# A two-block transformer kernel: norm sums joined, latent projections in full tiles, small tables loaded last

## What is computed

```python
# first block, each layer l
h = x @ w_in[l]                      # split into fox, latent (cq, ckv, kr), stick-breaking and windowed parts
q = (_rmsnorm(cq, g_q) @ w_uq).reshape(B, S, 4, 64 + 32)      # cq: 256 wide
kv = (_rmsnorm(ckv, g_kv) @ w_ukv).reshape(B, S, 4, 64 + 64)  # ckv: 128 wide
q = concat([q[..., :64], _rope(q[..., 64:], cos, sin)])       # then causal attention at scale 96 ** -0.5
y = _group_rmsnorm(mix, mix_g[l]) @ w_o[l]
x = _layernorm(ALPHA * x + y, ln1_g[l], ln1_b[l])
f = (silu(x @ w_gate[l]) * (x @ w_up[l])) @ w_down[l]         # 2816 wide
x = _layernorm(ALPHA * x + f, ln2_g[l], ln2_b[l])
# second block, each layer: half a SwiGLU, a mixer (differential attention with a bucketed
# relative bias, a short convolution, a gated linear recurrence), another half SwiGLU, RMS norms
```

## Time and profile before

| what | value |
|---|---|
| median of three runs | 3189.45 us (3188.94 to 3190.36) |
| the profiled execution's own time | 3188.79 us |
| its span | 3187.0 us |
| PE busy | 3149.3 us, 99% |
| POOL busy | 2284.4 us, 72% |
| DVE busy | 1169.8 us, 37% |
| ACT busy | 707.8 us, 22% |
| granted TensorE clock, mean | 0.998 |

### The profile page before, as it was taken

How to read it: one execution, slowest core, us unless ns; L and a number is a source line. 1 busy time by engine, 2 the same in 40 slices (tenths; PEclk the granted TensorE clock), 3 DMA queues, 4 the chain that set the end, 5 groups by cost and what they waited for, 6 DMA issues and landing times.

```text
span 3187.0 us, 45061 instructions
## 1 busy us (share of the span) xinstructions
PE 3149.3 (99%) x15738; PEld 2613.2 (82%) x15738; DVE 1169.8 (37%) x1874; ACT 707.8 (22%) x1444; POOL 2284.4 (72%) x3079
## 2 busy tenths in 40 slices
PE   8999999999999999999999999999999999999999
PEld 7778888887788888888888788888888887788887
DVE  5576111255761112542226552222222227542211
ACT  3453111044531110311102321110111012321100
POOL 5335877764358777598877478887888877398884
PEclk9999999999999999999999999999999999999999
DMA  5111322222113222232233122232322232132221
GB/s 182 47 41 60 112 93 98 96 90 67 41 54 106 98 98 93 71 108 95 96 99 103 60 80 99 99 99 93 99 92 99 99 109 86 41 106 99 93 98 66
DMA packets 83017, 284.08 MB, mean 89 GB/s; under 512 B 9531, under 2 KB 15068, under 8 KB 82652
## 3 DMA queue, kind: packets, MB, share of 16 engines
q1 hardware_dynamic: 77632, 274.76, 25.9%
q10 hardware_dynamic: 5276, 7.73, 0.7%
HBM read 278.79 MB, written 3.67 MB: 89 GB/s over the span
## 4 chain that ended last, share of the span: by engine, by line
PE 67%; POOL 19%; issue 13%; DVE 1%; POOLq 1%; ACT 0%; DMA 0%; SPq 0%; DVEq 0%; ACTq 0%
PE bank_v L512 14%; PE bank_v L514 14%; PE bank_v L513 14%; POOL w_lo L486 10%; PE bank_a L512 6%; PE bank_a L514 6%; PE bank_a L513 6%; POOL w_hi L484 6%; POOL zero L483 3%; PE bank_s L974 1%; PE bank_a L810 1%; PE bank_s L849 1%; PE bank_v L989 1%; PE bank_v L831 0%; PE bank_s L977 0%
## 5 line engine op out<-in xcount | busy, mean ns | idle before, releaser
L486 POOL TENSOR_TENSOR w_lo<-raw,w_hi 128x512 fp32r<-128x512 f32 x1024 | 1421.1, 1388 | 82.2
L483 POOL TENSOR_TENSOR zero<-zero 128x1 f32<-128x1 f32 x1024 | 288.8, 282 | 789.2 <-PE bank_v L514 606.8
L512 PE MATMUL bank_v<-xn_hi,w_hi 128*128 128x512 f32 (+1 forms) x1696 | 646.5, 381 | 14.4 <-DVE xn_lo L1640 12.1
L484 POOL CAST w_hi<-raw 128x512 fp32r<-128x512 f32 x1024 | 647.8, 633 | 0.0
L514 PE MATMUL bank_v<-xn_hi,w_lo 128*128 128x512 f32 (+1 forms) x1696 | 638.5, 376 | 0.0
L513 PE MATMUL bank_v<-xn_lo,w_hi 128*128 128x512 f32 (+1 forms) x1696 | 638.2, 376 | 0.0
L512 PE MATMUL bank_a<-xn_hi,w_hi 128*128 128x512 f32 (+1 forms) x1248 | 473.6, 379 | 8.4 <-DVE xn_lo L1640 5.4
L513 PE MATMUL bank_a<-xn_lo,w_hi 128*128 128x512 f32 (+1 forms) x1248 | 469.8, 376 | 0.0
L514 PE MATMUL bank_a<-xn_hi,w_lo 128*128 128x512 f32 (+1 forms) x1248 | 469.6, 376 | 0.0
L512 PE MATMUL bank_v<-h_hi,w_hi 128*128 128x512 f32 (+1 forms) x1122 | 423.7, 378 | 0.0
L513 PE MATMUL bank_v<-h_lo,w_hi 128*128 128x512 f32 (+1 forms) x1122 | 422.5, 377 | 0.0
(11 more groups left out here) (354 smaller groups left out, 3174.2 us busy)
## 6 DMA issues: line engine op xcount, KB each, us to landing
raw<-in_w_stream SPq DMA_DIRECT2D x516, 512.0 KB, 3.3
resid<-in_x SPq DMA_DIRECT2D x8, 256.0 KB, 9.1
rope<-in_rope ACTq DMA_DIRECT2D x2, 1024.0 KB, 6.1
da_v<-t_rows ACTq DMA_DIRECT2D x2, 1024.0 KB, 7.5
out<-resid SPq DMA_DIRECT2D x8, 256.0 KB, 2.3
t_rows<-t_row ACTq DMA_DIRECT2D x1, 1536.0 KB, 6.5
mla_v<-in_alibi ACTq DMA_DIRECT2D x2, 512.0 KB, 7.2
work<-in_lru_w ACTq DMA_DIRECT2D x2, 256.0 KB, 3.0
```

What stands on the lines that cost most here:

```text
L483: pool.tensor_tensor(zero[:, 1:2], zero[:, 0:1], zero[:, 0:1], ALU.add)
L484: pool.tensor_copy(w_hi[:, u, cut], raw[:, u, cut]).then_inc(*hi_split.done(("unit", u, n)))
L486: ins = pool.tensor_tensor(w_lo[:, u, cut], raw[:, u, cut], w_hi[:, u, cut].bitcast(F32), ALU.subtract)
L512: pe.matmul(out, lhs_hi, rhs_hi, start=first, stop=False)
```

## The change

It has five parts.

1. The six small tables are no longer issued by ACT at its start but by SP, behind the twelve loads of `HEAD` and ahead of the weight stream.
2. The weights of `uq` are laid out anew on the host, so that four outputs of 128 rows hold a head's 64 plain, 32 rotary and 32 turned rows; `uk` is formed as two outputs of two heads each. The scaling of the plain rows moves from DVE to ACT; DVE keeps cosine and sine for each head, and ACT copies both halves of each `uk` bank.
3. The shift is scaled by the matrix itself: `shift_weights` (-1/256, a memset of DVE at each norm) stands in place of `ones`, the operation L1802 is gone, and `base` and the centring of chunks 0 and 1 read the shift from PSUM.
4. For the first half DVE adds chunk 7 to both sums (two operations more, 128x256), and `ln_stats(tag, 0)` has four one-column matmuls in place of eight. The second half keeps its number.
5. Places: in `project_out` the spread of half 0 comes one step k (three matmuls) earlier; in `down` the sums of half 0 stand one step later (f = 4) and their spread one earlier (f = 8); in `project_halves` the second half's sums stand after n = 3 and its spread after n = 5. In the apply loop DVE's eviction of chunk 7's second half comes after step 4, and ACT's square of it after step 3.

```diff
-        ln_shift, ln_sum, ln_squares, ln_square = overlay(
+        shift_weights, _, ln_sum, ln_squares, ln_square = overlay(
...
+            for name, dest in (("rel", rel[0:BUCKETS, :]), ("rel_far", rel_far[0:BUCKETS, :]),
+                               ("bucket_of", bucket_of[0:BUCKETS + 1, :])):
+                sp.dma_start(dest, t[name]).then_inc(*rel_in.done(name, 16))
+            for name, dest in (("ident", ident[:, :]), ("mask", work[:, 0, 0:P]), ("strict", work[:, 0, P:2 * P])):
+                sp.dma_start(dest, t[name]).then_inc(*const_in.done(name, 16))
...
-                pe.matmul(bank_s[0][:, :], ones[:, :], work[:, 3, :], start=True, stop=True
+                pe.matmul(bank_s[0][:, :], shift_weights[:, :], work[:, 3, :], start=True, stop=True
...
-                late = tuple(c for c in (DC - 2, DC - 1) if s and c >= LN_HALVED[tag]) or (DC - 1,)
-                last = late[0] - 1
+                late = range(LN_HALVED[tag], DC) if s else ()
+                last = LN_HALVED[tag] - 1 if s else DC - 1
...
-                            if s == 1 and c == DC - 1 and k == 1:
+                            if s == 1 and c == DC - 1 and k == 0:
                                 ln_spread(tag, 0)
...
-                        if stats and s == 0 and n == 4:
+                        if stats and s == 0 and n == 3:
                             stats()
-                        if spread_factors and s == 0 and n == 7:
+                        if spread_factors and s == 0 and n == 5:
                             spread_factors()
...
-                            if s == 1 and f == 3 and norm != "final":
+                            if s == 1 and f == 4 and norm != "final":
                                 ln_stats(norm, 0)
-                            if s == 1 and f == 9 and norm != "final":
+                            if s == 1 and f == 8 and norm != "final":
                                 ln_spread(norm, 0)
...
-                for n in range(5):
+                for n in range(4):
                     b = v_bank(("uq", n))
...
-                for h in range(4):
-                    b = a_bank(("uk", h))
...
+                for p in range(2):
+                    b = a_bank(("uk", p))
+                    mm3(b[:, :], *w_tile(u, p), lat_hi[:, 2, :], lat_lo[:, 2, :], True, True).then_inc(*sums.done(("uk", p)))
...
-                apply(0, {0: lambda: square_of(DC - 2, 1) if late else None, 2: lambda: square_of(DC - 1, 1),
+                apply(0, {0: lambda: square_of(DC - 2, 1) if late else None, 3: lambda: square_of(DC - 1, 1),
...
-            for name, dest in (("rel", rel[0:BUCKETS, :]), ("rel_far", rel_far[0:BUCKETS, :]),
-                               ("bucket_of", bucket_of[0:BUCKETS + 1, :])):
-                act.dma_start(dest, t[name]).then_inc(*rel_in.done(name, 16))
...
-                    copy_bank(("uk", h), sums, mla_k[0:HD, h, :], rows=slice(0, HD))
+                    act.wait_ge(*(sums.after(("uq", h)) if h < 3 else w_used.after("uq")))
+                    act.activation(mla_q[0:HD, h, :], bank_v[v_read.slot(("uq", h), 2)][0:HD, :], ACT.Copy, scale=96.0 ** -0.5
+                                   ).then_inc(*act_step.done(("q_plain", h)))
+                for p in range(2):
+                    act.wait_ge(*sums.after(("uk", p)))
+                    act.activation(mla_k[0:HD, 2 * p, :], a_bank(("uk", p))[0:HD, :], ACT.Copy)
+                    copy_bank(("uk", p), sums, mla_k[0:HD, 2 * p + 1, :], rows=slice(HD, P))
...
-                    dve.scalar_tensor_tensor(out=resid[:, c, :], in0=resid[:, c, :], scalar=ALPHA, in1=ln_shift[:, :],
+                    dve.scalar_tensor_tensor(out=resid[:, c, :], in0=resid[:, c, :], scalar=ALPHA, in1=bank_s[0][:, :],
...
+                dve.memset(shift_weights[:, :], -1.0 / (2 * P)).then_inc(*dve_step.done((tag, "shift_weights")))
...
-                step(dve.tensor_scalar(ln_shift[:, :], bank_s[0][:, :], -1.0 / (2 * P), None, ALU.mult), (tag, "shift"))
...
+                        add_sum(DC - 1, 0)
+                        add_square(DC - 1, 0)
                 variance(0)
                 factors(0)
-                apply(0, {1: lambda: evict(DC - 2, 1) if late else None, 3: lambda: evict(DC - 1, 1),
+                apply(0, {1: lambda: evict(DC - 2, 1) if late else None, 4: lambda: evict(DC - 1, 1),
...
-                    dve.tensor_scalar(mla_q[0:HD, h, :], b[0:HD, :], 96.0 ** -0.5, None, ALU.mult
-                                      ).then_inc(*dve_step.done(("q_plain", h)))
-                    dve.tensor_tensor(mla_q[64:96, h, :], b[64:96, :], rope[64:96, 0, :], ALU.mult
+                    dve.tensor_tensor(mla_q[64:96, h, :], b[64:96, :], rope[64:96, 0, :], ALU.mult)
+                    dve.wait_ge(*act_step.after(("q_plain", h)))
+                    dve.tensor_tensor(work[64:96, h, :], b[96:128, :], rope[96:128, 1, :], ALU.mult
```

35 lines of the change are left out of this document (11 added, 24 removed).

## The result

The changed kernel took 3170.14 us (median of four runs, 3168.7 to 3172.25) against 3189.9 us for the kernel before (four runs, 3188.94 to 3193.68): a ratio of 0.994, with a 95% interval of 0.9928 to 0.9952. That is 19.8 us less; the forecast was 21.9 less, 3167, in a range of 3158 to 3179. The two spans differ by 20.4 us.

The account below looks back on a forecast made before the run. PE, busy 3149 of 3187 us, was taken to bound the kernel. Start 2.6, latents 4.6, ln1 9.6 and ln2 5.1 sum to 21.9; 3188.8 - 21.9 = 3166.9, said as 3167, range 3158 to 3179.

Parts of the forecast that it names:

- The start: Program start: tables moved off ACT bring head data 1.8 us sooner and faster matmuls 0.8 more; 2.6 us, bounds 0.5 to 4.
- the cover: At the start: six more issues on SP cost nothing, as ACT and POOL need them late; uncovered they cost 2.4 us.
- the 1.8 for the data: Program start: head data sooner by 1.8 us, from the tables' bytes (0.6) and the low rate, together at most 2.1.
- The latents: Latent projections: 12 matmuls fewer, 8.25 us work plus 2.5 stalls, 10.75 for 13.06; 2.3 a layer, 4.6 in all.
- The rival that nothing gets shorter: Latent projections: DVE's and ACT's copies pace them, so the part keeps its length; takes 4.6 back, 3171.5 us, chance 0.10.
- ln1: Norm ln1, two layers: first half gains 2.9 us, second half 1.9; 2 x 4.8 = 9.6.
- the first rival: First-half sums: POOL holds the new additions, 1.35 us each in place of 0.41; 3173 us, chance 0.14.
- With half as many I expect no fall: Behind ln1's first-half sums: four one-column matmuls, not eight, keep the clock at 1.00, saving 1.7 us.
- my own sign of being wrong: Wrong if waits for `xn_lo` only grow by what the sums give, or the lower clock moves to another place.
- ln2: Norm ln2: four sums fewer 0.9 a layer, second half's stalls 1.9 in layer 0, 1.4 in layer 1; 5.1 us.
- The slower rival: All four norms: PE waits at `ln_stats` for both additions behind POOL; 22 us lost against 14.3 gained, 3196.5, chance 0.02.
- The rival of several costs at once: Whole kernel: several of the first four rivals that cost come together, some 15 us less gain; 3182 us, chance 0.03.

Follow-up runs that it names:

- q on DVE: The changed kernel with the scaling of the four heads' plain rows back on DVE; latents 11.93 us in place of 10.46, span 3177.7 against 3166.6.

## Why the prediction was right, and where its steps were not

- **The start** (2.6 forecast, 1.3 measured). The direction and the cover were right: ident's cast moved up by itself to 18.71, and POOL, PE and ACT waited for no table. The term that was mis-sized is the 1.8 for the data: PE's last stand ended 0.73 sooner, and ACT stood 2.1 us for x1 where near 1 was to show it. The step that failed is that the low rate from 4 to 6 us was the tables' doing, "how small rows look". Without them it is 159 GB/s, as it was 156; with x on a second queue it is 287. I should have counted the tables' bytes, 0.6 us, and left the lost rate alone. The 0.8 for an earlier speed-up came on top, 0.6 of it, but by luck: the pace rose 1.8 sooner in this execution, and in others of the same start it rose as late as before.
- **The latents** (4.6, measured 5.2). The counts were right and the stalls mis-sized: 10.46 less 8.25 of work is 2.2 where I took 2.5. The rival that nothing gets shorter is out, but its argument was half true: the pace is that of the copies, as the run with q on DVE shows.
- **ln1** (9.6, measured 10.3). Split at the matmul that follows the second half's spread in the old order (300.51, 293.83 in the changed kernel), ln1 of layer 0 gained 2.8 and 2.3 where I had 2.9 and 1.9. `base` at 0.68, the two PSUM reads, the end of the sums and the place of the spread came as said: the spread at 276.19 is, with the 3.86 us gained by then, 280.05 of the old time, in the range of 279.7 to 280.3. Of the two additions one was held, 1.50, one not, 0.41: the first rival in half, and the joined sums are worth nothing at ln1, whereas I had counted four matmuls less as a gain there. The second half's places alone are worth 2.2 where I gave that half 1.9 in all. The rule of the Trainium skill ("SBUF — State Buffer", section "SBUF: two separate sides") agrees with both: 0.69 at most for `base` with one operand in PSUM, 1.52 for additions with two in SBUF.
- **The clock.** "With half as many I expect no fall" was right for the trace and wrong as a reason. Of 1.7 us a layer, I made a lasting gain; the runs show falls at the same norms with four sums and with eight, in three traces right behind the four. That the lower clock moves to another place was my own sign of being wrong, and it did. Part of the 5.1 of ln1 is of this kind: 324.08 less 1.5 for its one star is 322.6, which leaves 3.6 for the change itself. Undone one by one, the late places give 2.2 of it, the shift in PSUM 1.4, the joined sums -0.2 and the last eviction some 0.8; these make 4.2, so they overlap by some 0.6.
- **ln2** (5.1, measured 4.0). Layer 0 is as forecast, 3.2 for 2.8. In layer 1 the term was 2.3 and 0.8 came, because the clock fell there in this execution; in the runs that touch nothing in that part and have a shorter fall or none, it took 116.3 to 117.1, and the term would have been 1.6 to 2.4. The late places are worth 2.6 at ln2 of layer 0 and the joined sums 0.7, so 1.9 and 0.9 had the right order.
- **The slower rival** needed both additions held and a fall at all four norms. The wait of PE was 0.8 in place of the 3.8 it priced. **The rival of several costs at once** (3182) is out, and so is a result within 0.2%. The stalls behind the first half didn't vanish: each ln1 keeps two waits of 0.46 there, where one was of 1.25.
- **In the working itself** the upper bound of ln2, 7.2, has nothing behind it; its terms give 0.9 + 1.9 + 0.9 + 2.4 = 6.1. The chances that are to make 0.95 add up to 0.965. Neither moves the forecast.

That the spans' difference lies within 1.5 us of the sum owes something to errors that cancel: the start and ln2 were overrated by 2.4, the latents and ln1 underrated by 1.3. And it owes something to the execution that was profiled: with the falls at the norms where they were before, each ln1 would have given 1.5 less and ln2 of layer 1 some 1.2 more.

## What to carry to other kernels

When VectorE is the late engine beside a busy GpSimd, look at which of its operations have two operands in SBUF: an operand that can stay in PSUM is worth more than an operation saved, and an addition that is moved from TensorE to VectorE can cost as much as the matmuls it replaces. Where a matrix of ones is multiplied anyway, fold the scale into it. When a norm is worked in halves, try the places of the second half's sums first, for that was the largest piece measured here. And compare single traces part by part, at equal time of lower clock, before reading a difference of spans under some 4 us, since a fall of the clock can sit at another norm in the next execution.
